# First Fourier layer of a four-layer diffusion trunk: sequence transform ahead of the channel transform, on tokens normalised in their own layout, and eight modulation units moved into the first FFN

## What is computed

```python
def modulate(x, shift, scale):
    return rms_norm(x) * (1 + scale) + shift          # rms_norm has no gain

def fourier_mix(h, w_out):                            # real part of a 2-D DFT, over tokens and
    hg = h.reshape(B, T, 4, 256)                      # over the 256 channels of each of 4 groups
    f = jnp.fft.fftn(hg, axes=(1, 3), norm='ortho').real
    return f.reshape(B, T, D) @ w_out

mod = jax.nn.silu(cond) @ w_ada[i] + b_ada[i]         # (shift, scale, gate) twice, 6 x 1024
x = x + g1 * fourier_mix(modulate(x, sh1, sc1), w_fnet)
x = x + g2 * conv_ffn(modulate(x, sh2, sc2), w_ffn_in, w_ffn_conv, b_ffn_conv, w_ffn_out)
```

## Time and profile before

| | before |
|---|---|
| median of three runs | 2885.51 us |
| the profiled execution's own time | 2884.26 us |
| its span in the trace | 2882.5 us |
| PE busy | 2637.6 us (92%), 17182 matmuls |
| DVE busy | 1609.0 us (56%) |
| ACT, POOL busy | 917.0 us (32%), 846.6 us (29%) |
| granted TensorE clock, mean | 0.953 |
| bytes moved by DMA | 293.44 MB, mean 102 GB/s |

### The profile page before, as it was taken

One profiled execution on the slowest core, in us unless ns is written; L12 is line 12 of the kernel. 1 busy time (PEld: TensorE's weight loads), 2 busy tenths in 40 slices (PEclk: granted clock), 3 DMA queues, 4 the chain that ended last, 5 costly groups with the idle time before them and its releaser, 6 DMA issues.

```text
span 2882.5 us, 45477 instructions
## 1 busy us (share of the span) xinstructions
PE 2637.6 (92%) x17182; PEld 2589.7 (90%) x17182; DVE 1609.0 (56%) x2705; ACT 917.0 (32%) x1368; POOL 846.6 (29%) x414
## 2 busy tenths in 40 slices
PE   6889999996399999998888999999999888999997
PEld 6879999996399999988887889999999887999997
DVE  7478546576875475763543344754757776323235
ACT  3133223133332231343322333332323434323232
POOL 0012333334423333422111012233333302333332
PEclk9989999998699999999988899999999999999999
DMA  7433334342033343422100012333434311222222
GB/s 261 144 135 124 131 102 148 123 149 91 29 130 126 115 148 119 151 90 78 44 30 30 30 44 74 111 135 104 146 122 141 97 66 59 73 78 75 73 73 74
DMA packets 83858, 293.44 MB, mean 102 GB/s; under 512 B 9952, under 2 KB 13472, under 8 KB 83360
## 3 DMA queue, kind: packets, MB, share of 16 engines
q1 hardware_dynamic: 77184, 281.05, 28.9%
q10 hardware_dynamic: 6560, 10.79, 1.1%
HBM read 288.88 MB, written 2.93 MB: 101 GB/s over the span
## 4 chain that ended last, share of the span: by engine, by line
PE 63%; issue 16%; DVE 9%; POOL 5%; ACT 3%; DMA 2%; ACTq 0%; POOLq 0%; SPq 0%; DVEq 0%
PE acc L563 58%; POOL w_lo L441 4%; PE sacc L563 3%; PE sacc L784 2%; DMA raw<-in_stream 2%; DVE x L1760 1%; DVE rows L1789 1%; DVE pt_lo L1677 1%; POOL res_ffn L441 1%; DVE rows L1635 1%; POOL w_next L441 1%; DVE rows L1628 1%; DVE rows L1709 1%; DVE x L1700 1%; PE acc L980 1%
## 5 line engine op out<-in xcount | busy, mean ns | idle before, releaser
L441 POOL TENSOR_TENSOR w_lo<-raw,w_hi 128x1024 fp32r<-128x1024 f32 (+3 forms) x317 | 710.1, 2246 | 1729.4 <-ACT w_hi L1070 1729.4
L563 PE MATMUL acc<-h_hi,w_hi 128*128 128x322 f32 x2880 | 907.8, 315 | 90.9 <-DVE x L1780 28.6
L563 PE MATMUL acc<-h_lo,w_hi 128*128 128x322 f32 x2880 | 902.7, 313 | 0.0
L563 PE MATMUL acc<-h_hi,w_lo 128*128 128x322 f32 x2880 | 901.8, 313 | 0.0
L563 PEld LDWEIGHTS acc<-h_hi,w_hi 128*128 128x128 f32 x2880 | 549.6, 191 | 101.2 <-issue 77.4
L563 PEld LDWEIGHTS acc<-h_lo,w_hi 128*128 128x128 f32 x2880 | 552.5, 192 | 0.2
L563 PEld LDWEIGHTS acc<-h_hi,w_lo 128*128 128x128 f32 x2880 | 549.1, 191 | 0.0
L1070 ACT ACTIVATE w_hi<-raw 128x1024 fp32r<-128x1024 f32 (+2 forms) x283 | 293.0, 1036 | 784.7 <-PE acc L563 744.5
L1802 DVE SCALAR_TENSOR_TENSOR products<-raw,cond 128x1024 f32<-128x1024 f32 x324 | 440.5, 1396 | 12.2 <-ACT cond L1557 8.2
L1854 DVE SCALAR_TENSOR_TENSOR conv<-acc,conv_w,conv 128x644 f32<-128x644 f32 x168 | 149.4, 889 | 371.6 <-ACT conv L1293 267.8
L563 PE MATMUL acc<-g_hi,w_hi 128*128 128x322 f32 x1120 | 350.3, 313 | 5.8 <-POOL w_lo L441 5.8
(11 more groups left out here) (210 smaller groups left out, 3709.1 us busy)
## 6 DMA issues: line engine op xcount, KB each, us to landing
raw<-in_stream SPq DMA_DIRECT2D x536, 512.0 KB, 3.3
x<-in_x ACTq DMA_DIRECT2D x8, 322.0 KB, 10.2
cond<-in_cond ACTq DMA_DIRECT2D x2, 1024.0 KB, 5.8
inv_count<-in_inv_count ACTq DMA_DIRECT2D x1, 1328.0 KB, 5.7
out_y<-y ACTq DMA_DIRECT2D x2, 644.0 KB, 4.2
out_y<-y ACTq DMA_DIRECT2D x8, 161.0 KB, 2.5
rows<-in_rope ACTq DMA_DIRECT2D x1, 644.0 KB, 3.9
conv_w<-in_conv_w ACTq DMA_DIRECT2D x4, 88.0 KB, 2.3
```

The source lines that it names most:

```text
L441: done = nc.gpsimd.tensor_tensor(lo[:, cols], raw[slot][:, cols], hi[:, cols].bitcast(f32), ALU.subtract)
L563: done = nc.tensor.matmul(o, lhs[lp], rhs[rp][half], start=first and z == 0, stop=last and z == 2)
```

## The change

The token DFT comes first, the channel DFT second. Scale, shift and the reciprocal root mean square all commute with it in the right way: the root mean square belongs to a token and must be applied ahead of it, the scale is the same for all tokens of a group and can be applied behind it, and the shift, constant over tokens, only meets frequency zero.

- **Tokens in the stream.** Five new units carry `x` with tokens on partitions. ACT squares one with a row sum (`token_sum`), takes the root, DVE the reciprocal, ACT and DVE write `token_hi` and `token_lo`. The statistics by matmul, the normalisation and the scale into `h_hi`, `h_lo` and the 16 modulation units ahead of the first matmul are gone from this layer.
- **Stage 1** is now `token_tile(c, t)`: for each channel chunk c and token tile t six matmuls, of 258 and 256 columns for latent and of 66 and 64 for the context tile. Chunks 0 to 2 go tile by tile as the tiles arrive, chunks 3 to 7 chunk by chunk, with a modulation unit behind each. The eviction multiplies by the scale and writes `g_hi`, `g_lo` (`take_tokens`); column zero gets the shift apart (`zero_freq`).
- **Stage 2** contracts channels: eight results of 6 matmuls and the Nyquist result of 24, of 320 or 324 columns, with the four modulation units of the gate between the first.
- **Output projection** as before, but the modulation units of the second shift and scale (12 on PE, 4 on DVE) are now ahead of each turn's matmuls, where the 8 of the second gate on PE stood behind them.
- **The second gate's 8 units** go to the first FFN. Its stream has 56 instead of 48 units of modulation: 4 more in the projection of part 0 and 8 instead of 4 in that of part 1. 56 units now stand ahead of the FFN: 40 of modulation (26 on PE, 14 on DVE), 5 of tokens, 3 of tables, 8 to fold.
- **Loads on ACT's queue.** The small condition columns and biases come first, then the Nyquist row (512 KB, out of the stream); `cond` (1 MB) follows later, and the twelve loads of `x` and constants are issued by ACT between two token tiles.

The diff, cut to its core:

```diff
-ADA_EXTRA, EXTRA_PART = MODS - 2 * PAIRS, 1
-WEIGHT_PLACES, EXTRA_PLACES = [0, 1, 2, 3, 6, 7, 10, 11], [4, 5, 8, 9]
+EXTRAS = {0: {0: 4, 1: 8}, 1: {1: 4}, 2: {1: 4}}
+WEIGHT_PLACES = {4: [0, 1, 2, 3, 6, 7, 10, 11, 12, 13], 8: [0, 1, 4, 5, 8, 9, 12, 13, 16, 17]}
+T_ORDER = (1, 2, 3, 4, 0)
+C_ORDER = (5, 6, 7, 8, 0, 1, 2, 3, 4)
+def first_units():
+    units = [("token", 1), ("table", 0), ("table", 1), ("token", 2), ("token", 3), ("table", 2), ("token", 4),
+             ("token", 0)]
+    units += pe(*range(SC1, SC1 + 4))
+    for j in range(4):
+        units += pe(SC1 + 4 + j) + dve(SH1 + j)
+    units += dve(SH1 + 4, SH1 + 5) + pe(SH1 + 6, SH1 + 7)
+    for j in range(4):
+        units += dve(G1 + 4 + j) + pe(G1 + j)
+    units += [("fold", m) for m in range(3)]
     for m in range(KC):
-        units += [("fold", m)] + ([("pe", MODS - LAST_PE + m)] if late else [])
+        units += pe(SC2 + m) + (pe(SH2 + m // 2) if m % 2 == 0 else dve(SH2 + 4 + m // 2))
+        units += [("fold", m + 3)] if m + 3 < KC else []
     return units
...
+                for t in T_ORDER:
+                    if t == 3:
+                        wait_unit(first_place("table", 2))
+                    wait_unit(first_place("token", t))
+                    for c in range(3):
+                        token_tile(c, t)
+                    if t == 3:
+                        modulation(SC1, 0, 0)
+                    if t == 4:
+                        modulation(SC1 + 1, 0, 1)
+                modulation(SC1 + 2, 1, 0)
+                modulation(SC1 + 3, 1, 1)
+                for c in range(3, KC):
+                    pe.wait_ge(result_taken, c - 2)
+                    for t in T_ORDER:
+                        token_tile(c, t)
+                    if c < KC - 1:
+                        if c % 2:
+                            pe.wait_ge(mods_taken, c // 2)
+                        modulation(SC1 + 1 + c, (c + 1) // 2 % 2, (c + 1) % 2)
...
+                def late(m):
+                    if m == 0:
+                        pe.wait_ge(mods_taken, 5)
+                    modulation(SC2 + m, 0, m)
+                    if m % 2 == 0:
+                        modulation(SH2 + m // 2, 0, KC + m // 2)
...
+            def fold_project(layer, folds, following):
+                base = n.result
+                for m in range(KC):
+                    following(m)
+                    pe.wait_ge(folded_lo, folds + m + 1)
...
+                squares(3)
+                rounded(3)
+                first_table(2)
+                for c in range(KC):
+                    act.dma_start(x[:, c, :], a["x"][c]).then_inc(loaded, 16)
+                for dst, name in ((ident, "ident"), (ones, "ones"), (perm, "perm"), (gains, "gains")):
+                    act.dma_start(dst[:], a[name]).then_inc(loaded, 16)
+                squares(4)
...
+                for m in range(KC):
+                    following(m)
+                    update_folded(layer, m, base)
+                    if m + 2 < KC:
+                        fold_lo(m + 2, folds)
+                    if m + 3 < KC:
+                        fold_unit(place_(m + 3), m + 3)
+                    dve.wait_ge(summed, n.squared + m)
+                    add_square(row(SUM), n.squared + m, summed)
...
+                def late(m):
+                    if m % 2:
+                        unit(SH2 + 4 + m // 2)
```

More of the change, by code:

```diff
@@ L136, in fnet_units @@
     for m in range(KC):
-        units += [("fold", m)] + ([("pe", MODS - LAST_PE + m)] if late else [])
-    return units
-def fnet_place(layer, kind, first=0, last=MODS):
-    return [u for u, (k, i) in enumerate(fnet_units(layer)) if k == kind and first <= i < last]
+        units += pe(SC2 + m) + (pe(SH2 + m // 2) if m % 2 == 0 else dve(SH2 + 4 + m // 2))
+        units += [("fold", m + 3)] if m + 3 < KC else []
+    return units
+FIRST_UNITS = first_units()
+N_FIRST = len(FIRST_UNITS)
+FIRST_PE = [u for kind, u in FIRST_UNITS if kind == "pe"]
@@ L146, in extra, with first_place, fnet_units, fnet_place @@
+FIRST_DVE = [u for kind, u in FIRST_UNITS if kind == "dve"]
+FIRST_MODS = G2
+assert N_FIRST % SLOTS == 0 and len(FIRST_PE) + len(FIRST_DVE) == FIRST_MODS
+def first_place(kind, i):
+    return FIRST_UNITS.index((kind, i))
+def fnet_units():
+    return [("table", j) for j in range(TABLE_UNITS)] + [("nyquist", 0)] + [("fold", m) for m in range(KC)]
+def fnet_place(kind):
+    return [u for u, (k, i) in enumerate(fnet_units()) if k == kind]
 def extra(layer, part):
-    return ADA_EXTRA if ada_in_ffn(layer) and part == EXTRA_PART else 0
+    return EXTRAS.get(layer, {}).get(part, 0)
@@ L834, in fnet @@
                     for t in range(4):
-                        product([strip(i)[:, 0:near_cols]], lhs(t + 1), [[seq(p, t, odd)] for p in range(2)],
+                        product([strip(i)[:, 0:near_cols]], lhs(t + 1), [[seq_table(p, t, odd)] for p in range(2)],
                                 t == 0, t == 3)
@@ L1799, in modulate @@
                 wait_past(dve, ada_summed, count)
[L1800 removed]
+                out = products[slot % 2] if buffer is None else buffer
                 for z, signal in enumerate((ada_summed, unit_done[slot])):
@@ L1873, in ffn @@
                     if part == 0:
-                        pair(0, 0, acc)
-                        pair(1 // turn, 1 % turn, sacc[::-1])
-                    with dve.Fori(2 // turn if part == 0 else 0, count // turn) as i:
+                        pair(0, 0, acc, layer == 0)
+                        pair(1 // turn, 1 % turn, sacc[::-1], layer == 0)
+                    start = 2 // turn if part == 0 else 0
+                    if part == 0 and layer == 0:
+                        for i in range(2, (MODS - FIRST_MODS) // 2):
+                            pair(i, 0, acc, True)
+                        start = (MODS - FIRST_MODS) // 2
+                    with dve.Fori(start, count // turn) as i:
                         for z in range(turn):
@@ L2319, in _stream @@
                 if ada_in_ffn(layer):
-                    taken = 2 * p + extra(layer, EXTRA_PART) * (part > EXTRA_PART)
-                    out.append(ada[layer + 1][taken:taken + 2])
-            u = _weight_units(w_out[first * P:(first + count) * P])
-            taken = 2 * (first + count)
-            rest = ada[layer + 1][taken:taken + ADA_EXTRA] if extra(layer, part) else u[:0]
-            out += [u[:4], rest[:2], u[4:6], rest[2:], u[6:]]
+                    out.append(rest[taken:taken + 2])
+                    taken += 2
+            u, more = _weight_units(w_out[first * P:(first + count) * P]), extra(layer, part)
+            if not more:
+                out.append(u)
+                continue
+            units = np.empty((KC + more, P, UNIT), np.float32)
+            units[WEIGHT_PLACES[more][:KC]] = u
+            units[EXTRA_PLACES[more]] = rest[taken:taken + more]
+            out.append(units)
+            taken += more
     return np.concatenate(out)
```

722 lines of the change are left out of this document (434 added, 288 removed).

## The result

The changed kernel took 2875.25 us (median of 20 runs, 2858.48 to 2887.82) beside 2886.80 us of the kernel before (20 runs, 2873.74 to 2892.93): 0.4% faster, ratio 0.9960, 95% interval 0.9948 to 0.9973. A repetition on another occasion gave 2876.86 beside 2884.53, ratio 0.9972 (0.9960 to 0.9983). The forecast was 2889.0 and "same" (2876.9 to 2894.2), so the prediction was wrong: the change gains 8 to 12 us where I had it lose 3.5.

What follows compares the result with a forecast made beforehand. PE was taken to bound the kernel (busy 92%), its clock at half level around modulation units. Steps put the eighth turn's end at 196.7 against 193.2, 3.5 us later; with 2884.26 and 1.25 that gave 2889.0, range 2866 to 2901.

Steps and rivals of the forecast that it cites:

- start: Up to the first token product: condition columns, ACT's work on tile 1, POOL's table pieces; to 17.3 us, between 15 and 19.
- first three chunks: Token DFT, 17.3 to 49 us: half-level matmuls, ACT's twelve loads delaying tile 4, PE idle 4.4 us.
- five more chunks, five units: Token DFT, 49 to 83.9 us: a clock fall in nearly each chunk, 7.0 us a chunk, 34.9 in all.
- channel DFT and gate: 83.9 to 124.7 us: matmuls and modulation units at half level, with waits for landings; 8 us less at full level.
- turn 0: Output projection's first turn: 5.9 us, partly at half level, ending at 130.6.
- turns 1 to 4: Output projection: the stream sets the pace through DVE's buffer release; 21.0 us a pair of turns, 42.0 in all.
- turns 5 and 6: Output projection: 18.2 us, since the first unit has landed already.
- turn 7: Output projection's last turn: a unit of 1.84 and matmuls of 4.08 us, 5.9 in all, ending at 196.7.
- tail to the FFN: From the projection's last matmul to the FFN's first: 16.0 us, ended by the second `w_next` unit's landing, unchanged.
- first and second rivals: Clock stays up through all new stages (2850, chance 0.11), or only among chunks and first products (2874, chance 0.14).
- the third: Output projection: the stream decides, landings take 5.6 us, a pair of turns 26 instead of 21; 2906, chance 0.25.
- faster: Whole kernel: a time below the "same" band of 2876.9 to 2894.2 us; chance 0.25.

Runs made afterwards that it cites:

- the thinned kernel: Each first-layer modulation unit on PE issues one matmul of its eight, against the changed kernel: 2847.13 us, ratio 0.9881.

## Why the prediction was wrong

The forecast's steps against two profiles of the changed kernel (length of each in us):

| step | forecast | after | repeated |
|---|---|---|---|
| start | 17.3 | 15.7 | 15.8 |
| first three chunks | 31.7 | 30.9 | 28.9 |
| five more chunks, five units | 34.9 | 32.7 | 35.5 |
| channel DFT and gate | 40.8 | 40.6 | 40.6 |
| turn 0 | 5.9 | 4.1 | 4.1 |
| turns 1 to 4 | 42.0 | 40.9 | 40.8 |
| turns 5 and 6 | 18.2 | 16.2 | 18.9 |
| turn 7 | 5.9 | 5.8 | 5.8 |
| tail to the FFN | 16.0 | 15.1 | 15.1 |
| first FFN matmul at | 212.7 | 201.9 | 205.5 |

**Most of the mechanisms held.** A fall of the clock in nearly each chunk, the half level through the channel DFT, the queue's wait for the buffer behind DVE's sums, an FFN that takes eight units more for nothing: each was found in the trace, and the falls among the chunks, the wait and the FFN were each shown by a run as well. The first and second rivals (the clock stays up) and the third (26 us a pair) had nothing for them.

**Two paths were drawn wrong, where the length came out near.** The gap at 25 to 29 us is there (3.85 us, forecast 4.4), but it was not ended by ACT. PE waited for the landing of the modulation unit, which took 7.3 to 8.2 us beside the twelve loads. ACT's path was only the next behind it: DVE finished the low part of tile 4 at 30.7 us, the unit ended at 31.9, and with the unit thinned PE did wait for tile 4, until 29.7. And the first pair of turns took 20.0 us, forecast 21.0, by another route: I had turn 1 at 5.9 us and then 2.7 of idle. Turn 1 took 8.9 (1.34 of waiting, then matmuls partly at half level), and there was no idle behind it. That the pair came out right is luck. The next pair is made as forecast: its units start 8.5 us after the turn before, where I had 8.6.

Of the Trainium skill ("TensorE: Matmul & The Clock Gate", "What's actually happening"): by its rule the clock follows idleness and sustained work. Here it fell in chunks in which PE had no idle time at all (32.70 busy in 32.70 us, granted 0.80), and with seven of eight matmuls of each unit left out the last four of these five chunks held 1.00. The measurement decides against the rule as I read it.

**The step that failed is the sum: its terms were mis-sized, all on one side.** On the mean of the two profiles they are 9.0 us too long: the first three chunks 1.8, turn 0 1.8, the start 1.6, turns 1 to 4 1.1, the tail 0.9, five chunks 0.8, turns 5 and 6 0.6, the rest 0.3. Later profiles, in which these stages are as in the changed kernel, tell a wrong price from chance:

- *Start:* 17.3 forecast, 15.5 to 16.0 in all ten.
- *Tail:* 16.0 forecast, 14.7 to 15.3 in all but the thinned kernel.
- *Turn 0:* 5.9 forecast, "partly half level". The Nyquist row's 24 matmuls ahead of it had brought the clock up, and it ran at 4.1 in six of nine profiles, at 5.6 in three.
- *Turns 1 to 4:* 42.0 forecast, 38.9 to 40.9 in the four profiles with the fold sums and the units as in the changed kernel.
- *First three chunks:* no wrong price. They took 34.2, 28.7 and 33.8 us in three more profiles, so the mean of five is 31.3 beside the 31.7 forecast. A unit and the short matmuls behind it take 4.0 us when the clock is up and 7.1 when it is down (5.8 forecast), and that is chance. ACT issued the loads from 19.5 to 26.45 us and not by 28; it made no difference here, since the unit's landing ended the gap.

So start, turn 0, turns 1 to 4 and tail are the steps to name, 5.4 us together. None of them alone would have turned the forecast.

**A term was put at nothing.** The sum let all that follows the first FFN's first matmul stand as it was. It is 2.8 us shorter (2302.5 and 2303.4 before, 2301.0 and 2299.3 after, 2294.6 to 2301.0 in all ten profiles with the new order). The cause stays open.

**The base was a point, taken as fixed.** The 193.2 and 209.2 of before came from one execution; a second gave 212.8. Its mean is 1.8 us later. 9.0 and 1.8 are the 10.8 between +3.5 forecast and -7.3 measured at the first FFN matmul; with the 2.8 behind it that makes -10. The range (2866 to 2901) held the time; the chances did not weigh that the base itself moves by 3.6 us, where 12.1 separate the forecast from "faster".

**What the argument lacked was a price for the second part by itself.** The prediction said that the gate's eight units "is in the stages above". Priced alone from its own rows, it is four units of PE at 1.84 to 3.43 in the projection, 7 to 14 us, and the run that undid it gave 12 to 15 in the stage. The reordering would then have stood as what it is, a move that only breaks even. With all units in place its projection begins 25 us earlier (120.6 us, 145.3 and 146.2 before) and takes 81.5 us instead of 47.9 and 50.3.

## What to carry to other kernels

Price each part of a change by itself, even if one sum covers them: a free move (units into an engine-bound stage with 1.00 of PE and half of DVE) can carry a reordering that brings nothing. Then run each part alone, on the old kernel too. Where a queue issues in order over few buffers, look at which engine frees each buffer and at what place of its own turn: moving 1.3 us of sums ahead of an update took 6 to 10 us out of eight turns in three profiles and 13 or more in one, and 9.5 us off the time, about as much as the whole change. And take a second profile of the base before a forecast of less than 0.5% is made against it.

## What the runs showed of the hardware

The granted clock of unchanged code differs from run to run: attention took 359.5 us at 0.91 and 375.5 at 0.86. Over the 20 runs of the changed kernel the fastest (2858.5 us) had a mean clock of 0.947 and the slowest (2887.8) 0.937, so that most of their spread goes with the clock. Chunk 3 began, with nothing edited ahead of it, at 44.6 to 46.6 us in three profiles and at 49.7 and 49.8 in two, in which the granted clock had fallen at 27.4 and 27.8 us and not at 29.2 to 30.2.

The loads of one queue delayed another queue's transfers: beside the twelve loads of ACT the stream's units took 7.3 to 8.2 us from issue to landing (6.4 to 7.3 in the repeated profile), and with the loads moved away 3.2 to 4.4 in the same stretch. These are the rows of the issues between 20 and 24 us in the changed kernel, with the median time to landing last:

```profile
x<-in_x ACTq DMA_DIRECT2D x7, 322.0 KB, 7.6
raw<-in_stream SPq DMA_DIRECT2D x2, 512.0 KB, 7.8
```
